# One core, a hybrid decoder layer: the loads of down's weights move from SyncE's queue to ScalarE's

## The chip, the cores and the metric

The kernel runs on one core of one Trainium2 chip. The metric is the device time of one execution in microseconds (us), lower is better. A profiled execution gives the trace from which all rows below come. A core has five engines with queues of their own: TensorE (PE), VectorE (DVE), ScalarE (ACT), GpSimd (POOL) and SyncE (SP); 16 DMA engines move data between the chip's memory (HBM) and the core's SBUF. A transfer is issued by an instruction in an engine's queue, here SP's or ACT's.

## The reference, cut to what matters

One layer on 256 tokens of width 1024: an SSD mixer, cross-attention into 256 memory rows, and a mixture of 32 experts, of which each token uses 4. The change touches the experts alone:

```python
def expert_block(args):
    xb, e = args
    gu = xb @ w_gate_up[e] + b_gate_up[e]            # 1024 x 2048 weights
    gate = jnp.minimum(gu[..., :D_FF], SWIGLU_LIMIT)
    up = jnp.clip(gu[..., D_FF:], -SWIGLU_LIMIT, SWIGLU_LIMIT)
    act = (up + 1.0) * (gate * jax.nn.sigmoid(gate * SWIGLU_ALPHA))
    return act @ w_down[e] + b_down[e]               # 1024 x 1024 weights
```

The rows of an expert's output are scaled by the router's gates and added to the tokens they belong to. All is float32: 8 MB of gate-up and 4 MB of down weights for each expert, 403 MB for the 32.

## The kernel before, in words

The mixer and the attention fill roughly the first 390 us. Their weights come in 2 MB pieces through three slots. Then come the 32 experts, one after the other, each with up to 64 tokens ("slots"); for experts with more than 64 tokens there is a list of extra rounds, which these inputs don't use.

Expert weights go through a ring of twelve 1 MB buffers in SBUF: eight for gate-up (`GP`), each with 128 rows of 8 KB, and four for down (`DP`), each with 256 rows of 4 KB. `load_gate_up` and `load_down` (lines 306 and 309) issue one piece each; landing raises a semaphore of that buffer, `g_ready[s]` or `d_ready[s]`. PE raises `gu_used` and `dn_used` after the last matmul of each piece, and that frees the buffer.

PE's order for expert e (`regular`, lines 788 to 798) is: transpose of the scatter matrix (line 714), gate_up(e) over eight pieces (726), gather of the tokens of e+1 (706), down(e-1) over four pieces (750), transposes of the gate-up sums of e (737), scatter of e-1 (760). So down runs one expert behind gate-up. down(e-1) needs `act` of e-1 and the scatter matrix in SBUF.

SP's loop (lines 361 to 364) follows the same order: the eight pieces of gate-up for the next expert, each as soon as the present expert's matmuls have freed its buffer, then the four pieces of down, each as soon as the piece of the expert before has been used. `wait_ge` stands before every issue, and the queue is served in order.

ACT's order for an expert (`regular`, lines 1044 to 1051) is: scatter matrix out of PSUM (`scatter_out`), the gate half of the sums (`gate_out`), the next expert's tokens (`tokens_out`), the former expert's down sums (`down_out`, which waits for all four of its pieces through `dn_used`), and the sigmoid of this expert. All are recorded as line 826, the helper's. ACT issues four small transfers at the start of the kernel and none later. DVE does the other half of the sums (1381), the clamps and products of SwiGLU (1388 to 1400, the last waits for the sigmoid) and the one-hot matrices.

```python
def reload_down(e, i, c):
    for s in range(DP):
        sp.wait_ge(dn_used, 2 * DP * i + (DP * (c - 1) + s + 1))
        load_down(sp, e, s)
```

Of the kernel before, what the change touches and what calls it, by code (L numbers as in the profile page):

```python
# [43 lines left out]
NE, TOPK = 32, 4  # L44
# [4 lines left out]
PAIRS = NE // 2  # L49
# [6 lines left out]
GP, DP = 8, 4  # L56
# [4 lines left out]
def build(nc, x, mem, mixer_norm, xattn_norm, mem_norm, ffn_norm, w_in, conv_w, conv_b, dt_bias, a_log,  # L61
          d_skip, ssd_norm, w_out, xa_w_q, xa_w_kv, xa_w_o, w_router, b_router, w_gate_up, b_gate_up,
          w_down, b_down, final_norm, out):
    with ExitStack() as ctx:
# [187 lines left out]
        def used(n):  # L252

            if n < W_Z:
                return u_ps, 2 * (n - W_U) + 2
            if n < KV_PIECE[0]:
                return z_ps, 2 * (n - W_Z) + 2
            if n in KV_PIECE:
                return kv_ps, 2 * KV_PIECE.index(n) + 2
            if n < W_Q:  # L260
                return wo_ps, (1, 2, 5, 6)[n - W_OUT]
            return (q_ps, 2 * (n - W_Q) + 2) if n < W_O else (wo_ps, 9 + n - W_O)
# [27 lines left out]
        def wpiece(n):  # L290
            return wslot[n % 3].rearrange("p (k n) -> p k n", k=KD)
# [7 lines left out]
        def dn_w(s):  # L299
            return slot(GP + s).rearrange("p (k n) -> p k n", k=2)  # L300
# [4 lines left out]
        def load_gate_up(sp, e, s):  # L305
            sp.dma_start(gu_w(s), gu_dram[e, s, :, :]).then_inc(g_ready[s], 16)  # L306

        def load_down(sp, e, s):
            sp.dma_start(dn_w(s), dn_dram[e, s, :, :, :]).then_inc(d_ready[s], 16)  # L309
# [4 lines left out]
        @block.sync  # L314
        def _(sp):
            for t in range(TC):
                sp.dma_start(h[:, t, :], x[P * t:P * (t + 1), :]).then_inc(ld_x, 16)
            for r0, v in ((16, mem_norm), (24, ssd_norm)):
                n = v.shape[0] // P
                sp.dma_start(rows_b[r0:r0 + n, :], v.rearrange("(c p) -> c p", p=P)).then_inc(ld_rows, 16)  # L320
            sp.wait_ge(ld_rows, 96)
            sp.dma_start(wpiece(0), pieces[0]).then_inc(w_ready[0], 16)
            sp.dma_start(wdt[:, :, :], w_in[:, 5120:5152].rearrange("(k p) n -> p k n", p=P)).then_inc(ld_wdt, 16)
            for n, v in enumerate((dt_bias, a_log, d_skip)):
                sp.dma_start(small[:, n, :], v.partition_broadcast(P)).then_inc(ld_small, 16)
            sp.dma_start(b_rt[:, :], b_router.partition_broadcast(P)).then_inc(ld_small, 16)
            sp.dma_start(bg_rows, b_gate_up.rearrange("e (f q) -> (e f) q", q=P).rearrange(
                "(n p) q -> p n q", p=P)).then_inc(ld_bg, 16)
            sp.dma_start(wpiece(1), pieces[1]).then_inc(w_ready[1], 16)
            sp.dma_start(vb[:, :, :], mem.rearrange("(t p) d -> p t d", p=P)).then_inc(ld_mem, 16)  # L330
            sp.dma_start(wpiece(2), pieces[2]).then_inc(w_ready[2], 16)
            sp.dma_start(wrt[:, :, :], w_router.rearrange("(k p) n -> p k n", p=P)).then_inc(ld_wrt, 16)
            for n in range(3, len(pieces)):
                signal, count = used(n - 3)
                sp.wait_ge(signal, count)
                sp.dma_start(wpiece(n), pieces[n]).then_inc(w_ready[n % 3], 16)
            sp.wait_ge(sc_ps, XH)
            sp.dma_start(g_ffn, ffn_norm.partition_broadcast(P)).then_inc(ld_g, 16)
            sp.wait_ge(pT_ps, XH)
            for s in range(GP):  # L340
                load_gate_up(sp, 0, s)
            sp.wait_ge(wo_ps, 10)
            for s in range(DP):
                load_down(sp, 0, s)
            sp.dma_start(bdn[0:NE, :], b_down).then_inc(ld_bdn, 16)
            sp.dma_start(g_fin, final_norm.partition_broadcast(P)).then_inc(ld_gf, 16)

            def reload_gate_up(e, i, c):

                for s in range(GP):  # L350
                    sp.wait_ge(gu_used, 2 * GP * i + (GP * (c - 1) + s + 1))
                    load_gate_up(sp, e, s)
# [7 lines that stand above are left out]
            reload_gate_up(1, 0, 1)  # L360
            with sp.Fori(0, PAIRS - 1, 1) as i:
                for c in range(2):
                    reload_gate_up(2 * i + (c + 2), i, c + 2)
                    reload_down(2 * i + (c + 1), i, c + 1)
            reload_down(NE - 1, PAIRS - 1, 1)
            sp.wait_ge(lst_ok, 1)
            extra = sp.value_load(lst_i[0:1, 32:33], min_val=0, max_val=MAX_EXTRA)
            with sp.Fori(0, EXTRA_PAIRS, 1) as q:
                with sp.If(extra > 2 * q):
                    for c in range(2):  # L370
                        e = sp.value_load(lst_i[0:1, ds(2 * q + (16 + c), 1)], min_val=0, max_val=NE - 1)
                        reload_gate_up(e, q, NE + c)
                        reload_down(e, q, NE + c)
            for t in range(TC):
                sp.wait_ge(o_ok, t + 1)
                sp.dma_start(out[P * t:P * (t + 1), :], h[:, t, :]).then_inc(ld_out, 16)
            sp.wait_ge(ld_out, 16 * TC)
# [446 lines left out]
        def _(act_):  # L824
            def fn(out_, in_, func, **kw):
                return nc.scalar.activation(out_, in_, func, **kw)  # L826
# [179 lines left out]
            def tokens_out(i, c, buf):  # L1006

                act_.wait_ge(gathered, 2 * i + (c + 1))
                fn(xs[:, buf, :, :], ps[3][:, :].rearrange("p (k s) -> p k s", k=KD), ACT.Copy).then_inc(xs_ok, 1)

            def scatter_out(i, c):

                act_.wait_ge(st_ps, 2 * i + (c + 1))
                fn(scatT[:, :], ps[2][:, 0:SEQ], ACT.Copy).then_inc(sT_ok, 1)

            def gate_out(i, c):

                act_.wait_ge(gu_used, 2 * GP * i + GP * (c + 1))
                fn(gus[:, 0:512], ps[0][:, :], ACT.Copy).then_inc(gus_act, 1)

            def sigmoid(i, c):

                act_.wait_ge(gate_b, 2 * i + (c + 1))
                fn(sg[:, :, :, :], gu[:, 0, :, :, :], ACT.Sigmoid, scale=ALPHA).then_inc(sg_ok, 1)

            def down_out(i, c):

                act_.wait_ge(dn_used, 2 * DP * i + DP * (c + 1))
                fn(ysb[:, :], ps[2][:, :], ACT.Copy).then_inc(y_ok, 1)
# [14 lines left out]
            def regular(i, c, buf, more=True):  # L1044

                scatter_out(i, c)
                gate_out(i, c)
                if more:
                    tokens_out(i, c + 1, 1 - buf)
                down_out(i, c - 1)  # L1050
                sigmoid(i, c)

            with act_.Fori(0, PAIRS - 1, 1) as i:
                regular(i, 1, 1)
                regular(i, 2, 0)
            regular(PAIRS - 1, 1, 1, False)
            scatter_out(PAIRS - 1, 2)
            down_out(PAIRS - 1, 1)
# [434 lines left out]
```

## Time and profile before

| what | value |
|---|---|
| time, median of 3 runs | 1374.69 us (1371.0 to 1376.38) |
| the profiled execution | 1370.06 us |
| its span, first to last instruction | 1368.3 us |
| PE busy | 1278.7 us, 93% of the span |
| DVE, ACT, POOL busy | 380.2, 247.4, 18.8 us |
| DMA | 454.24 MB, mean 332 GB/s |
| gate-up issues on SP | 256 of 1024 KB, median 20.1 us to landing |
| down issues on SP | 128 of 1024 KB, median 24.4 us to landing |
| mean granted TensorE clock | 0.98 |

The profile is one execution. Its own time differs from its span by what lies around the first and the last instruction, 1.8 us. Busy time counts an engine's instructions; waits, and the issues of transfers, are not in it. The time to landing runs from the start of the issue to the moment at which the whole piece has arrived.

### The profile page before, as it was taken

The numbers are of one execution on the slowest core, as the hardware profiler recorded it, in microseconds if no ns is written. First come the engines' busy times: TensorE is split into PE (matmuls) and PEld (weight loads), VectorE is DVE, ScalarE is ACT, GpSimd is POOL, SyncE is SP. The second block draws the span as 40 slices with busy tenths as digits, with TensorE's granted clock in tenths as the row PEclk, the third lists the DMA queues.
The fourth block names the chain that finished last, engine by engine and source line by source line (L and its number), as shares of the span: only waits on it lengthen the run. The fifth ranks groups of instructions, "written<-read, shape, count | busy, mean of one in ns | idle before, by whom it ended". The sixth has DMA issues, their size and how long they took to land.

```text
span 1368.3 us, 17022 instructions
## 1 busy us (share of the span) xinstructions
PE 1278.7 (93%) x6566; PEld 684.3 (50%) x6566; DVE 380.2 (28%) x746; ACT 247.4 (18%) x389; POOL 18.8 (1%) x33
## 2 busy tenths in 40 slices
PE   6999998989899999999999999999999999999984
PEld 6998775867654444444433433333344343333421
DVE  1885577343421121112111111211111122111112
ACT  2754225233301010001000000100000010000101
POOL 1000210000000000000000000000000000000000
PEclk9999999999878999999999999999999999999997
DMA  8454213332857999999999999999999999999993
GB/s 290 161 184 175 73 62 123 123 123 102 356 208 310 417 417 416 418 419 419 418 418 416 416 417 418 419 419 418 416 417 416 418 419 418 418 417 417 416 416 133
DMA packets 99187, 454.24 MB, mean 332 GB/s; under 512 B 9364, under 2 KB 10036, under 8 KB 66388
## 3 DMA queue, kind: packets, MB, share of 16 engines
q1 hardware_dynamic: 98976, 453.75, 82.3%
q8 instruction: 21, 0.34, 0.1%
q10 hardware_dynamic: 180, 0.07, 0.0%
q14 instruction: 10, 0.08, 0.0%
HBM read 452.74 MB, written 1.05 MB: 332 GB/s over the span
## 4 chain that ended last, share of the span: by engine, by line
PE 45%; DMA 32%; SPq 16%; DVE 3%; issue 2%; ACT 1%; DVEq 1%; ACTq 0%
DMA ring<-in_moe_w_gate_up 28%; PE ps L726 11%; SPq L306 9%; PE ps L750 6%; SPq L309 6%; PE ps L706 5%; PE ps L485 3%; PE ps L486 3%; PE ps L487 3%; PE ps L576 2%; PE ps L500 2%; PE ps L502 2%; PE ps L501 2%; DMA ring<-in_moe_w_down 2%; PE ps L580 1%
## 5 line engine op out<-in xcount | busy, mean ns | idle before, releaser
L726 PE MATMUL ps<-ring,wring 128*64 128x512 f32 x2048 | 464.9, 601 | 35.0 <-DMA ring<-in_moe_w_gate_up 33.4
L726 PEld LDWEIGHTS ps<-ring,wring 128*64 128x64 f32 x2048 | 142.0, 137 | 336.2 <-issue 230.2
L750 PE MATMUL ps<-ring,wring 128*64 128x512 f32 x1024 | 227.4, 596 | 3.7 <-DMA ring<-in_moe_w_down 2.5
L826 ACT ACTIVATE wring<-ps 128x512 f32<-128x512 f32 (+1 forms) x133 | 72.2, 544 | 832.5 <-PE ps L726 486.0
L1381 DVE COPY wring<-ps 128x512 f32<-128x512 f32 x32 | 22.1, 692 | 431.9 <-PE ps L726 431.9
L750 PEld LDWEIGHTS ps<-ring,wring 128*64 128x64 f32 x1024 | 70.4, 137 | 135.6 <-issue 121.5
L1388 DVE TENSOR_TENSOR wring<-ps,bguT 128x512 f32<-128x512 f32 x64 | 44.0, 688 | 332.6 <-PE ps L737 332.6
L706 PEld LDWEIGHTS ps<-wring 128*128 128x128 f32 x1024 | 120.0, 196 | 26.7 <-issue 25.2
L706 PE MATMUL ps<-wring 128*128 128x64 f32 x1024 | 124.4, 281 | 1.4 <-DVE wring L1367 1.4
L1117 DVE TENSOR_TENSOR wlo<-wring,lo_ring 128x2048 fp32r<-128x2048 f32 x26 | 58.8, 2288 | 41.9 <-ACT lo_ring L826 41.9
L760 PE MATMUL ps<-wring 64*128 64x512 f32 x256 | 63.6, 615 | 0.7 <-ACT wring L826 0.7
L826 ACT ACTIVATE lo_ring<-wring 128x2048 fp32r<-128x2048 f32 x26 | 49.0, 1916 | 34.4 <-DMA wring<-in_ssd_w_in 16.8
L502 PE MATMUL ps<-hi_ring,wlo 128*128 128x256 f32 x192 | 54.4, 283 | 0.0
L500 PE MATMUL ps<-hi_ring,lo_ring 128*128 128x256 f32 x128 | 36.6, 286 | 5.3 <-DVE act_lo L1281 3.5
L737 PEld LDWEIGHTS ps<-cst,wring 128*128 128x128 f32 x256 | 28.1, 143 | 25.2 <-issue 25.1
L486 PE MATMUL ps<-wlo,hi_ring 128*128 128x512 f32 x96 | 38.2, 398 | 0.0
L502 PEld LDWEIGHTS ps<-hi_ring,wlo 128*128 128x128 f32 x192 | 36.9, 192 | 0.0
L485 PE MATMUL ps<-lo_ring,hi_ring 128*128 128x512 f32 x80 | 32.6, 407 | 4.2 <-DVE hi_ring L1306 4.2
L737 PE MATMUL ps<-cst,wring 128*128 128x128 f32 x256 | 35.8, 284 | 0.0
L760 PEld LDWEIGHTS ps<-wring 64*128 64x128 f32 x256 | 22.1, 186 | 21.8 <-issue 20.3
L473 PE MATMUL ps<-mid,wring 128*128 128x256 f32 x128 | 29.5, 393 | 2.2 <-DMA wring<-in_ssd_w_in 2.2
L1184 DVE SCALAR_TENSOR_TENSOR ring<-ps,parT,ring 128x255 f32<-128x255 f32 (+2 forms) x72 | 31.1, 477 | 1.8
(234 smaller groups left out, 1067.9 us busy)
## 6 DMA issues: line engine op xcount, KB each, us to landing
ring<-in_moe_w_gate_up SPq DMA_DIRECT2D x256, 1024.0 KB, 20.1
ring<-in_moe_w_down SPq DMA_DIRECT2D x128, 1024.0 KB, 24.4
wring<-in_ssd_w_in SPq DMA_DIRECT2D x10, 2048.0 KB, 8.0
wring<-in_xa_w_kv SPq DMA_DIRECT2D x4, 2048.0 KB, 8.2
wring<-in_ssd_w_out SPq DMA_DIRECT2D x4, 2048.0 KB, 7.7
wring<-in_xa_w_q SPq DMA_DIRECT2D x2, 2048.0 KB, 7.9
wring<-in_xa_w_o SPq DMA_DIRECT2D x2, 2048.0 KB, 10.4
h<-in_x SPq DMA_DIRECT2D x2, 512.0 KB, 4.3
```

Of the source, the lines that this page charges most:

```text
L306: sp.dma_start(gu_w(s), gu_dram[e, s, :, :]).then_inc(g_ready[s], 16)
L309: sp.dma_start(dn_w(s), dn_dram[e, s, :, :, :]).then_inc(d_ready[s], 16)
L485: mm(ps[bank][:, :], xh[:, k0 + k, tok], wh, start=start and k == 0, stop=False)
L486: mm(ps[bank][:, :], xh[:, k0 + k, tok], wl, start=False, stop=False)
L500: mm(dst, wh[:, c0:c0 + P], x_hl[0][:, k, :], start=k == 0, stop=False)
L502: last = mm(dst, wl[:, c0:c0 + P], x_hl[0][:, k, :], start=False, stop=k == KD - 1)
L706: last = mm(ps[G_BANK][:, SLOTS * k:SLOTS * (k + 1)], xn[:, t, P * k:P * (k + 1)], onehot[:, buf, t, :], start=t == 0, stop=t == TC - 1)
L726: last = mm(ps[a][SLOTS * half:SLOTS * (half + 1), :], xs[:, buf, s, :], w[:, c0:c0 + 512], start=s == 0, stop=s == GP - 1)
L737: last = tr(ps[a][:, P * j:P * (j + 1)], gus[:, c0:c0 + P], ident)
L750: last = mm(ps[D_BANK][SLOTS * half:SLOTS * (half + 1), :], act[:, k, :], w[:, kk, 512 * half:512 * (half + 1)], start=k == 0, stop=k == K ...
L760: mm(ps[4 + 2 * half + t][:, :], scatT[r, P * t:P * (t + 1)], ysb[r, :], start=False, stop=True, skip_group_check=True)
L826: return nc.scalar.activation(out_, in_, func, **kw)
```

## The change

SP no longer issues the pieces of down in its main loop, and neither those of the last expert behind it. ACT issues them: behind `down_out` of expert e-1, and before the sigmoid of e, it issues the four pieces of down for e, without a wait of their own, since `down_out` has already waited until all four buffers are free. The first expert's down pieces and those of the extra rounds stay with SP.

```diff
@@ -361,8 +361,6 @@
             with sp.Fori(0, PAIRS - 1, 1) as i:
                 for c in range(2):
                     reload_gate_up(2 * i + (c + 2), i, c + 2)
-                    reload_down(2 * i + (c + 1), i, c + 1)
-            reload_down(NE - 1, PAIRS - 1, 1)
             sp.wait_ge(lst_ok, 1)
             extra = sp.value_load(lst_i[0:1, 32:33], min_val=0, max_val=MAX_EXTRA)
             with sp.Fori(0, EXTRA_PAIRS, 1) as q:
@@ -1048,6 +1046,8 @@
                 if more:
                     tokens_out(i, c + 1, 1 - buf)
                 down_out(i, c - 1)
+                for s in range(DP):
+                    load_down(act_, 2 * i + c, s)
                 sigmoid(i, c)
 
             with act_.Fori(0, PAIRS - 1, 1) as i:
```

## Rows read from the trace of the kernel before

**Rows 1.** The page's part 2, share of the DMA engines in 40 slices of the span.

```profile
DMA  8454213332857999999999999999999999999993
```

**Rows 2.** Windows of the span: length, busy us (instructions) of each engine, PEclk, DMA share, GB/s.

```profile
450.05:700.00 249.95, 248.35 (x1297) 108.52 (x1297) 45.56 (x99) 24.96 (x45) 0.00 (x0) 1.00 1.02 418
700.00:1000.00 300.00, 284.88 (x1456) 118.80 (x1454) 50.62 (x110) 28.05 (x50) 0.00 (x0) 1.00 1.02 418
```

**Rows 3.** PE's timeline, 440 to 482 us: start, length, line, operation, tiles, count.

```profile
442.63 7.09 PE L750 MATMUL ps<-ring,wring 128*64 128x512 f32 x32
...
453.01 13.95 PE L726 MATMUL ps<-ring,wring 128*64 128x512 f32 x64
466.89 3.79 PE L706 MATMUL ps<-wring 128*128 128x64 f32 x32
470.61 7.09 PE L750 MATMUL ps<-ring,wring 128*64 128x512 f32 x32
```

**Rows 4.** PE's timeline, 815 to 850 us; in brackets idle time before and what ended it.

```profile
827.58 8.80 PE L726 MATMUL ps<-ring,wring 128*64 128x512 f32 x40
836.77 1.94 PE L726 MATMUL ps<-ring,wring 128*64 128x512 f32 x8 [0.39 <-DMA ring<-in_moe_w_gate_up]
839.26 1.94 PE L726 MATMUL ps<-ring,wring 128*64 128x512 f32 x8 [0.56 <-DMA ring<-in_moe_w_gate_up]
...
847.32 3.23 PE L750 MATMUL ps<-ring,wring 128*64 128x512 f32 x14
```

**Rows 5.** SP's line 309 from 786 to 803 us: issue ns min/median/max, and landing.

```profile
L309 SPq DMA_DIRECT2D ring<-in_moe_w_down x4: 488/3654/4412, 789.3 to 798.8; - x4
...
DMA to landing us min/median/max: 23.1/24.9/25.8
```

**Rows 6.** SP's timeline, 440 to 482 us.

```profile
455.13 12.33 SPq L306 DMA_DIRECT2D ring<-in_moe_w_gate_up  x8
472.72 5.52 SPq L309 DMA_DIRECT2D ring<-in_moe_w_down  x4
```

**Rows 7.** Single issues at 397.5, 439.2 and 444.8 us, each with its landing.

```profile
L306 SPq DMA_DIRECT2D ring<-in_moe_w_gate_up x1: 334/334/334, 397.5 to 397.5; - x1
...
DMA to landing us min/median/max: 4.7/4.7/4.7
...
L306 SPq DMA_DIRECT2D ring<-in_moe_w_gate_up x1: 332/332/332, 439.2 to 439.2; - x1
...
DMA to landing us min/median/max: 10.9/10.9/10.9
...
L309 SPq DMA_DIRECT2D ring<-in_moe_w_down x1: 384/384/384, 444.8 to 444.8; - x1
...
DMA to landing us min/median/max: 7.9/7.9/7.9
```

**Rows 8.** ACT's timeline, 815 to 850 us.

```profile
824.37 0.60 ACT L826 ACTIVATE wring<-ps 128x512 f32<-128x512 f32 x1 [6.43 <-PE ps L750]
826.29 0.63 ACT L826 ACTIVATE wring<-wring 128x512 f32<-128x512 f32 x1 [1.33 <-DVE wring L1392]
827.67 0.38 ACT L826 ACTIVATE wring<-ps 128x256 f32<-128x256 f32 x1 [0.74 <-PE ps L714]
843.72 0.60 ACT L826 ACTIVATE wring<-ps 128x512 f32<-128x512 f32 x1 [15.67 <-PE ps L726]
```

**Rows 9.** DMA queues between 3 and 4 us (q1 SyncE's, q10 ScalarE's): packets, MB, share.

```profile
q1 hardware_dynamic: 97, 0.36, 88.9%
q10 hardware_dynamic: 98, 0.04, 15.0%
```

**Rows 10.** PE's timeline, 1296 us to the end.

```profile
1299.12 7.09 PE L750 MATMUL ps<-ring,wring 128*64 128x512 f32 x32
...
1323.85 1.94 PE L726 MATMUL ps<-ring,wring 128*64 128x512 f32 x8 [0.54 <-DMA ring<-in_moe_w_gate_up]
1326.49 1.94 PE L750 MATMUL ps<-ring,wring 128*64 128x512 f32 x8 [0.71 <-DMA ring<-in_moe_w_down]
...
1334.08 1.94 PE L750 MATMUL ps<-ring,wring 128*64 128x512 f32 x8 [0.62 <-DMA ring<-in_moe_w_down]
...
1340.55 7.09 PE L750 MATMUL ps<-ring,wring 128*64 128x512 f32 x32 [1.22 <-DVE wring L1400]
```

## Prediction, before the changed kernel ran

> **What bounds the kernel now.** Below, G(e) and D(e) are the eight gate-up and the four down pieces of expert e, 1 MB each, and "down(e)" is the stretch of matmuls that uses D(e). I read the page's row of DMA shares first: from the thirteenth slice to the last but one every digit is 9 [rows 1]. The windows then give 1.02 as the share and 418 GB/s as the rate, both before 700 us and after it, while PE falls from all but 1.6 us of the first window to 284.88 of 300 us [rows 2]. So the transfers don't stop at 700 us, but PE starts to wait there.
>
> PE's timeline shows the two regimes. Early, one expert takes PE 477.70 - 449.72 = 28.0 us between the ends of two downs: 3.3 of small work, 13.95 gate-up, 3.7 gather, 7.1 down, without a gap [rows 3]. Later the gate-up matmuls come in bursts 2.49 us apart, each released by a DMA [rows 4]. At the end down does the same, (1334.08 - 1326.49) / 3 = 2.53 us apart [rows 10]; I take 2.55 for a down piece. One expert's bytes thus take 8 x 2.49 + 4 x 2.55 = 19.9 + 10.2 = 30.1 us, 2.1 more than PE's 28.0. **The bound is the DMA engines, busy without a pause from before 450 us [rows 2] until the last expert's down.** Whatever the change does to the order of the bytes costs nothing by itself; what costs is a pause of the engines.
>
> SyncE looks like a bottleneck but isn't one. In the bound regime a down piece holds its queue for a median of 3.65 us and lands 23.1 to 25.8 us after its issue [rows 5], while early, with fewer pieces ahead, an issue takes 0.38 us [rows 7]. The queue is simply full; nobody waits for the issue, since 23 us are some nine pieces that lie ahead of each.
>
> **The change, part by part.** Removed: 31 x 4 waits and issues on SP. SP now issues G alone, at most eight pieces outstanding, so its 3.65 us stalls go. I cost this at nothing: a G piece that enters a full queue earlier lands no earlier. If the queue were ever empty it would be worth up to the stall.
>
> Added: 124 issues on ScalarE. In each expert four stand after the down eviction and before the sigmoid. On an unfilled queue four take 4 x 0.38 = 1.5 us [rows 7]; on a full one up to 4 x 4.4 = 17.6 us [rows 5]. Now ACT evicts at 824.37, does the sigmoid at 826.29 and is next needed at 827.67 and 843.72 [rows 8]. With 1.5 us nothing moves. What waits behind it: the sigmoid, DVE's last product, and with it act for down, whose matmuls start 23 us after the eviction [rows 4]; then scatT, for the same down; then the gate half's eviction at 843.72. The long bound would end at 842.6 and leave 1.1 us for a sigmoid and an eviction that take 1.0, so even it would barely show. I take 1.5 us and nothing on the path, for ACT's queue never holds more than four pieces.
>
> Delayed: D. Piece 0 goes out today at 472.72, 2.1 us after down starts, and the four within 5.5 us, the last just after the end [rows 3, 6]. After the change all four wait for the end T of down, the semaphore (0.1) and the eviction (0.60 [rows 8]). A piece on an empty queue lands 4.7 us after issue [rows 7], 2.5 of it transfer, so 2.2 is start-up. D's bytes thus begin to move at T + 0.7 + 2.2 = T + 2.9. (If ScalarE's queue issues before the eviction ends it is T + 2.3.) That matters only where less than 2.9 us of gate-up transfer is queued at T; call this remainder x.
>
> *Head.* T = 449.72 for expert 0. G(2) has all landed at 439.2 + 10.9 = 450.1, so x = 0.4, and D(1) piece 0 lands today at 444.8 + 7.9 = 452.7, straight behind it [rows 7]. Afterwards it lands at T + 2.9 + 2.55 = 455.2. **Cost 2.5 us**, once: from the next expert on x grows by 2.1 each time.
>
> *Middle.* Two queues now feed the same DMA engines, and today's timeline shows how they share in one microsecond only: between 3 and 4 us, ScalarE's queue moved 98 packets and SP's 97 [rows 9], though SP's carried 0.36 MB and the other 0.04. So turns, not bytes, are equal. What a turn holds for G and D is not shown. A G row is 8 KB, a D row 4 KB, which by single rows gives G two bytes for each of D; if a turn is as many bytes for both, they go equal. The Trainium skill's DMA: Bandwidth & Descriptors, Queues, rings and completion order, says that an engine goes round-robin between queues and drains a whole packet of several descriptors each time; by it no order of issue is kept between SP and ScalarE, and the equal counts above agree. Its section Issuing engines are not separate DMA queues says that spreading issues gains no bandwidth; by it the sum has no gain. If the packet of the first section were all that one piece gives an engine, the same 64 KB for both, that rule would mean equal shares and the 1384 below; no run shows how large it is here.
>
> Two to one: D needs 3 x 10.2 = 30.6 us while G is queued. G(e+2) pieces are asked for from 2.1 us after gate-up starts [rows 3, 6] and can move from T + 3.3 + 2.1 + 2.2 = about T + 7.7. From x = 5: G runs dry at 2.9 + 2.1 x 1.5 = 6.1, D runs alone to 7.7, has had 2.7 and ends at 7.7 + 3 x 7.5 = 30.2; the last down piece ends at 32.1; G(e+2) has had 15.0 + 1.9, so x = 19.9 - 16.9 = 3.0. From x = 3: D ends at 24.2, PE needs its 28.1, and x = 5.0 again. Rounds of 32.1 and 28.1 average 30.1: the engines stay fed, barely, as 3.0 is just over 2.9. Equal shares: D lands by T + 23.3, G's last at T + 2x - 2.9, and the next T is 1.9 + 3.7 + 7.1 later, T + 2x + 9.8; for rounds of 30.1, x = 10.1. Either way **the middle costs nothing**, but PE now waits for D or for G in place of running ahead, and x falls.
>
> *Tail.* Here the small x is paid. Expert 29's down ends today at T29 = 1299.12 + 7.09 = 1306.2, G(31) is complete at 1323.8, so x = 17.6; down(30) ends at 1336.0 and down(31) at 1347.6, 11.6 later, partly waiting for DVE [rows 10]. Afterwards D(31) can't be asked for before T30: it is complete at T30 + 0.7 + 2.2 + 10.2 = 13.1 and used 1.9 later, at T30 + 15.0, 3.4 more than today, with the engines idle. And T29 comes later, since more bytes must have moved by then. With two to one (x about 4): T29 = 1306.2 + 2.5 + 13.6 = 1322.3; then PE's own 3.3 + 13.95 + 7.1 = 24.4 gives T30 = 1346.7, and down(31) ends at 1361.7: **14.1 us late**. With equal shares (x = 10.1): T29 = 1316.2, T30 = 26.4 later (G(31) lands at T29 + 17.3, no gather), 1342.6, end 1357.6: 10.0 late.
>
> **The sum**: 2.5 in the head, 0 in the middle, 11.6 in the tail (8.2 from x, 3.4 from the late D(31)). On the profiled execution's 1370.06 us (span 1368.3) that gives 1384.2. The three runs shown have their median 4.6 above the profiled one; I keep most of that and say **1388 us**, against a median of 1374.69. I take two to one, because the row sizes are what the trace has; equal shares would give 1384.
>
> **Rivals.** *1, the middle starves as well.* With two to one every second round has x = 3.0 against 2.9. A slower start-up, or a G share above two, makes x fall short, and the engines pause up to 2.9 us in each of some 22 late rounds, or D lands so late that down waits longer than G(e+2), with only eight slots, can fill. At 0.7 to 1.4 us a round: 15 to 31 more, 1403 to 1419. For it: the margin of 0.1. Against it: a longer round also refills x.
>
> *2, order kept.* If older requests were served first, G(e+1) would stay ahead of D(e), x would stay 17.6, and only 2.5 + 3.4 = 5.9 us would be lost: 1380. Against it the equal counts of rows 9.
>
> *3, faster.* A D piece takes 0.06 us longer than a G piece for the same bytes, with 16 rows for each of the 16 engines where G has 8; so a row seems to cost 0.06 / 8 us beyond its bytes, 0.06 for G and 0.12 for D. If another queue's work hid that cost entirely, a G piece would take 2.43 and a D piece 2.43, and an expert 29.2: 0.9 x 31 = 28 less than the forecast, or 1360. It decides where the round is shorter than 30.1 by 14.1 / 30 = 0.5 us, that is above 425 GB/s where rows 2 show 418. Against it: the share is 1.02 already. The same place could also lose: a rate 1% lower costs 9 us.
>
> *4, nothing happens.* If D's issue landed in time in head and tail for a reason not seen, or other effects gave 11 us back, the time stays near 1375.
>
> **How the numbers follow.** About 0.5% (7 us) is what a measurement of this kernel can tell from no change, so the border is 1381.6. Forecast, with shares from equal to two to one: 0.53, 1382 to 1394. Starved middle, or a lower rate: 0.25, all slower. Order kept: 0.11, on the border, halved. Faster: 0.05. Nothing: 0.06. That makes slower 0.83, same 0.12, faster 0.05. The range leaves out the faster case, most of the unchanged one and the far end of the starved one: 1379 to 1412.
>
> **What would show it.** D issues on ACTq of about 0.4 us each, and no SP issue over 1 us. Middle windows still at 1.0 and 418 GB/s. D(1) piece 0 landing near 455. At T29 only 3 to 10 us of G(31) left, D(31) issued after T30 and landing 10 to 13 us later, with a DMA gap between. Wrong if: down matmuls in the middle are never later than gate-up's data (order kept); the middle's rate is below 415 or above 425; or ACT's issues take 4 us each and its evictions slip.

## The result, and the profile after

The changed kernel takes 1387.89 us, the median of four runs (1385.43 to 1390.18), against 1374.99 for the kernel before (also four): a ratio of 1.0098, 95% interval 1.0071 to 1.0126. In a second comparison with more runs (E1 below) it is 1.0122 (1.0103 to 1.0140). So the change costs about 1%, 13 to 17 us. The difference of the medians and the one by the ratio lie up to 1.3 us apart in the experiments below, which give both. The profiled execution took 1385.43 us against 1370.06, its span is 1383.6 us against 1368.3: 15.3 longer. In the new kernel the gate-up matmuls have line 724 and down's 748, two less than before.

First the page of the changed kernel: DMA shares by slice, then the queues (packets, MB, share).

```profile
DMA  8455123333857999999999999999999999999973
...
q1 hardware_dynamic: 65248, 323.71, 57.9%
q10 hardware_dynamic: 33908, 130.10, 23.6%
```

The row of nines answers to [rows 1]; its last digit but one is a 7 now, where the kernel before had a 9: the engines run dry before the end. q10 is ScalarE's queue: 130 MB of down weights have moved there. Next the windows, with the columns of [rows 2]:

```profile
450.00:700.00 250.00, 237.44 (x1202) 102.47 (x1200) 44.86 (x98) 23.94 (x43) 0.00 (x0) 0.97 1.00 410
700.00:1000.00 300.00, 286.38 (x1462) 124.06 (x1460) 50.62 (x110) 28.03 (x50) 0.00 (x0) 0.97 1.02 417
1000.00:1300.00 300.00, 284.19 (x1457) 122.78 (x1455) 49.34 (x106) 28.05 (x50) 0.00 (x0) 0.98 1.02 418
```

From 700 us on the DMA engines are as busy as before, 417 and 418 GB/s. Before 700 us they lose some: 410 instead of 418. The prediction named a middle rate below 415 as a sign of being wrong. This window also holds the pause of the head (14 GB/s between 450 and 452 us); from 490 to 700 us alone the rate is 413, so in these first rounds there are short pauses that the prediction did not have. Then ACT's timeline and the issues of both queues:

```profile
1022.50 0.60 ACT L824 ACTIVATE wring<-ps 128x512 f32<-128x512 f32 x1 [6.43 <-PE ps L748]
1022.63 1.99 ACTq L309 DMA_DIRECT2D ring<-in_moe_w_down  x4
1024.67 0.63 ACT L824 ACTIVATE wring<-wring 128x512 f32<-128x512 f32 x1 [1.57 <-DVE wring L1392]
```

```profile
L306 SPq DMA_DIRECT2D ring<-in_moe_w_gate_up x81: 332/333/333, 699.7 to 999.9; - x81
```

Four issues take ACT 2.0 us, and no SP issue takes over 0.333 us, where a down piece held SP for a median of 3.65 [rows 5]. The first issue starts at 1022.63, 0.13 us after the eviction began and before its end at 1023.10: here the queue does not wait for the engine to finish. The sigmoid keeps its place behind DVE's line 1392, about as in [rows 8].

How the pieces land: three issues of ScalarE's queue in one expert, and PE beside them.

```profile
L309 ACTq DMA_DIRECT2D ring<-in_moe_w_down x3: 379/379/380, 1023.2 to 1024.2; - x3
...
DMA to landing us min/median/max: 13.0/19.9/26.7
```

```profile
997.76 13.96 PE L724 MATMUL ps<-ring,wring 128*64 128x512 f32 x64
...
1015.36 7.09 PE L748 MATMUL ps<-ring,wring 128*64 128x512 f32 x32
...
1025.71 13.96 PE L724 MATMUL ps<-ring,wring 128*64 128x512 f32 x64
...
1043.31 5.37 PE L748 MATMUL ps<-ring,wring 128*64 128x512 f32 x24
1050.97 1.94 PE L748 MATMUL ps<-ring,wring 128*64 128x512 f32 x8 [2.30 <-DMA ring<-in_moe_w_down]
```

The three were issued at 1023.17, 1023.71 and 1024.24 and landed 13.0, 19.9 and 26.7 us later: at 1036.2, 1043.6 and 1050.9, so 7.4 and 7.3 us apart, three times the 2.49 of a gate-up piece. While both queues have work, from 1040 to 1050 us, they move nearly as many packets as each other, and SyncE's twice the bytes:

```profile
q1 hardware_dynamic: 375, 2.81, 67.4%
q10 hardware_dynamic: 365, 1.40, 35.1%
```

In exchange gate-up, which PE waited for in [rows 4], now comes in time: 13.96 us without a gap in both rounds. PE waits for down's last piece instead, 2.30 us here. The ends of down stand at 1022.45 and 1052.91: a round of 30.5, and the one before, 994.50 to 1022.45, is 27.95. And the end of the kernel, which answers to [rows 10]:

```profile
1316.69 7.09 PE L748 MATMUL ps<-ring,wring 128*64 128x512 f32 x32
...
1327.02 13.96 PE L724 MATMUL ps<-ring,wring 128*64 128x512 f32 x64
1340.80 7.04 PE L748 MATMUL ps<-ring,wring 128*64 128x512 f32 x32
...
1353.07 5.35 PE L748 MATMUL ps<-ring,wring 128*64 128x512 f32 x16 [1.92 <-DMA ring<-in_moe_w_down]
1358.76 1.94 PE L748 MATMUL ps<-ring,wring 128*64 128x512 f32 x8 [0.34 <-DMA ring<-in_moe_w_down]
1361.27 1.94 PE L748 MATMUL ps<-ring,wring 128*64 128x512 f32 x8 [0.57 <-DMA ring<-in_moe_w_down]
```

down(29) ends at 1323.78, 17.6 us later than before, down(30) at 1347.84, 11.8 later, and down(31) at 1363.20, 15.6 later. down(31) is now served piece by piece from the DMA engines, 15.4 us behind down(30), where it took 11.6 and waited only for its activations. D(31) is issued from 1347.9 us on, and from 1342 to 1346 us nothing moves (0 GB/s): that pause is the 7 in the row of shares.

### The profile page after: what moved, and what is told of

Same layout as the page of the kernel before. It is cut to its first block, busy times and chain, and to the rows that moved or that the text cites. A ratio compares the mean times of both kernels' runs of the same rounds, so it can differ in the third digit from the quotient of the medians.

```text
span 1383.6 us, 16904 instructions
## 1 busy us (share of the span) xinstructions
PE 1288.1 (93%) x6566; PEld 698.9 (51%) x6566; DVE 380.3 (27%) x746; ACT 247.3 (18%) x389; POOL 18.8 (1%) x33
## 4 chain that ended last, share of the span: by engine, by line
PE 61%; DMA 31%; DVE 3%; ACTq 2%; issue 1%; ACT 1%; SPq 1%; DVEq 1%
DMA ring<-in_moe_w_down 29%; PE ps L724 18%; PE ps L748 12%; PE ps L704 5%; PE ps L483 3%; PE ps L484 3%; PE ps L485 3%; PE ps L758 2%; PE ps L574 2%; PE ps L498 2%; PE ps L499 2%; PE ps L500 2%; PE ps L735 2%; ACTq L309 1%; DMA wring<-in_ssd_w_in 1%
## 5 line engine op out<-in xcount | busy, mean ns | idle before, releaser
L724 PEld LDWEIGHTS ps<-ring,wring 128*64 128x64 f32 x2048 | 149.2, 138 | 280.6 <-issue 280.0
L748 PEld LDWEIGHTS ps<-ring,wring 128*64 128x64 f32 x1024 | 72.3, 143 | 187.2 <-issue 124.1
L735 PE MATMUL ps<-cst,wring 128*128 128x128 f32 x256 | 38.8, 300 | 0.0
## 6 DMA issues: line engine op xcount, KB each, us to landing
ring<-in_moe_w_gate_up SPq DMA_DIRECT2D x256, 1024.0 KB, 14.1
wring<-in_xa_w_o SPq DMA_DIRECT2D x2, 2048.0 KB, 10.3
```

Source lines behind the costliest of these rows:

```text
L724: last = mm(ps[a][SLOTS * half:SLOTS * (half + 1), :], xs[:, buf, s, :], w[:, c0:c0 + 512], start=s == 0, stop=s == GP - 1)
L735: last = tr(ps[a][:, P * j:P * (j + 1)], gus[:, c0:c0 + P], ident)
L748: last = mm(ps[D_BANK][SLOTS * half:SLOTS * (half + 1), :], act[:, k, :], w[:, kk, 512 * half:512 * (half + 1)], start=k == 0, stop=k == K ...
```

## The experiments

Two explanations were set against each other. The main one is that of the prediction: two queues share the DMA engines, so that down takes bytes that gate-up needs first, and x (the gate-up transfer still queued at the end of a down) falls; that is paid for once, at the end, together with a late start in the head and a late D(31). The rival: it is the late issue that costs, in each round, and the second queue is harmless.

### E1: the changed kernel again

No edit.

> The changed kernel once more, as the measure for the three beside it. Main theory (D's own queue shares two to one with gate-up, so that the gate-up queued at the end T of a down, x, falls from 17 us to 2 to 9 us; this is paid once at the end, with 2.5 us in the head and 3.4 for the late D(31)): 13 to 16 us over the kernel before, rounds of 28 to 35 us averaging 30.1. Rival (D issued late starves the DMA engines in every round): the same total, but windows of the middle below 415 GB/s.

Measured: 1389.04 us against 1371.71, 17.3 us more; ratio 1.0122 (1.0103 to 1.0140), which is 16.7. That is just over the upper end of 13 to 16. The rounds of its trace lie between 27.9 and 34.7 us; from the end of down(9) at 722.31 to that of down(29) at 1327.54 they average 605.23 / 20 = 30.26. The rival wanted windows of the middle below 415 GB/s: they show 418 (700 to 1000 us) and 417 (1000 to 1300 us). Only the window from 450 to 700 us, which holds the head's pause, shows 411.

### E2: late, but in one queue

The edit is on `reload_down` of the kernel before.

```diff
-                for s in range(DP):
-                    sp.wait_ge(dn_used, 2 * DP * i + (DP * (c - 1) + s + 1))
-                    load_down(sp, e, s)
+                sp.wait_ge(dn_used, 2 * DP * i + DP * c)
+                for s in range(DP):
+                    load_down(sp, e, s)
```

> SP issues everything as in the kernel before, but the four pieces of D(e) all wait until the last piece of down(e-1) is used. One queue, so order is kept. Main theory: only head (2.5) and D(31) (3.4) are lost, 5 to 7 us over the kernel before; rounds stay at 30.1 each, x stays 17.4. Rival (late issue is the whole loss): 13 us or more, as with the change.

Measured: 1380.04 us, 8.3 us more; ratio 1.0051 (1.0032 to 1.0070), which is 7.0. That is the upper end of 5 to 7, or just over it. PE's timeline at the end:

```profile
1307.16 7.09 PE L750 MATMUL ps<-ring,wring 128*64 128x512 f32 x32
...
1326.74 1.94 PE L726 MATMUL ps<-ring,wring 128*64 128x512 f32 x8 [0.44 <-DMA ring<-in_moe_w_gate_up]
1329.42 1.94 PE L726 MATMUL ps<-ring,wring 128*64 128x512 f32 x8 [0.74 <-DMA ring<-in_moe_w_gate_up]
1331.91 1.94 PE L726 MATMUL ps<-ring,wring 128*64 128x512 f32 x8 [0.55 <-DMA ring<-in_moe_w_gate_up]
...
1342.07 1.94 PE L750 MATMUL ps<-ring,wring 128*64 128x512 f32 x8 [0.55 <-DMA ring<-in_moe_w_down]
...
1349.15 1.94 PE L750 MATMUL ps<-ring,wring 128*64 128x512 f32 x8 [1.83 <-DMA ring<-in_moe_w_down]
...
1357.37 1.94 PE L750 MATMUL ps<-ring,wring 128*64 128x512 f32 x8 [0.57 <-DMA ring<-in_moe_w_down]
```

The middle is that of the kernel before: the last gate-up pieces come 2.5 to 2.7 us apart, released by the DMA, the round from 1314.25 (end of down(29)) is again DMA-bound, and down(30) ends 29.8 later. down(31) ends at 1359.31, 15.3 behind down(30) instead of 11.6: **3.7 us for the late D(31)**. In the head, between 440 and 490 us, 19.71 MB moved instead of 20.88, which is 2.8 us. The late issue alone is worth no more than half of the change's loss: 8.3 of 17.3 us by the medians, 7.0 of 16.7 by the ratios. The rival, which wanted 13 us or more, falls.

### E3: two queues, nothing late

```diff
-                down_out(i, c - 1)
                 for s in range(DP):
+                    act_.wait_ge(dn_used, 2 * DP * i + (DP * (c - 1) + s + 1))
                     load_down(act_, 2 * i + c, s)
+                down_out(i, c - 1)
```

The eviction `down_out` now stands behind the four issues.

> ACT issues D, each piece as soon as its own buffer is free, ahead of the eviction. Two queues, nothing late. Main theory: no loss in the head, none for D(31); x still falls to about 4, so T29 comes 17.6 - 4 = 13.6 late and the last round is 5.4 shorter: 7 to 9 us over the kernel before, with D landings 7.3 us apart while gate-up is queued. Rival (late issue is the whole loss): within 2 us of the kernel before.

Measured: 1377.52 us, 5.8 us more; ratio 1.0036 (1.0023 to 1.0049), which is 4.9. That is below the 7 to 9 expected and outside the rival's 2. The four D pieces issued from 1008.0 to 1013.5 land from 11.5 to 27.8 us after their issues, 7.3 us apart as expected. PE at the end:

```profile
1312.93 1.94 PE L748 MATMUL ps<-ring,wring 128*64 128x512 f32 x8 [0.47 <-DMA ring<-in_moe_w_down]
...
1333.56 7.04 PE L748 MATMUL ps<-ring,wring 128*64 128x512 f32 x32
...
1345.12 7.09 PE L748 MATMUL ps<-ring,wring 128*64 128x512 f32 x32 [1.05 <-DVE wring L1401]
```

down(29) ends at 1314.87, 8.7 later than in the kernel before, the next round takes 25.7 instead of 29.8, and down(31) follows after 11.6, as before, at 1352.21: 4.6 late, of which 0.4 were there at the end of down(0), and the rest comes from the bytes that moved earlier than they were needed. After T29 12.91 MB are left here, 16.16 in the kernel before: 3.25 MB, or 7.8 us, make down(29) late, and the shorter round gives 4.1 of them back. The mechanism is as expected, its size was not: I had carried x = 4 over from the late case. With D issued during the former down, D is well on its way at T. The last gate-up piece still lands 16.9 us after T here, two thirds of which are its own transfer: x = 11.3.

### E4: the change, with D(31) early

```diff
+            reload_down(NE - 1, PAIRS - 1, 1)
             sp.wait_ge(lst_ok, 1)
...
-                for s in range(DP):
+                for s in range(DP if more else 0):
                     load_down(act_, 2 * i + c, s)
```

> The changed kernel, but D(31) alone is issued by SP again, each piece as soon as its buffer is free. Main theory: down(31) ends 11.6 us after down(30) instead of 15.4, so 3 to 4 us less than the changed kernel, 10 to 12 over the kernel before; T30 unchanged. Rival (down(31) is bound by its activations and not by D(31)): no gain.

Measured: 1383.80 us, 12.1 over the kernel before; ratio 1.0086 (1.0072 to 1.0100), which is 11.8; and 5.2 below E1, which was measured beside it.

```profile
1340.93 7.04 PE L749 MATMUL ps<-ring,wring 128*64 128x512 f32 x32
...
1352.50 7.09 PE L749 MATMUL ps<-ring,wring 128*64 128x512 f32 x32 [1.22 <-DVE wring L1401]
```

down(30) ends at 1347.97, within 0.2 of the changed kernel's, and down(31) 11.6 later, at 1359.59, no longer 15.4: 3.8 us, where the sum had 3.4. The rival (no gain) falls. The medians say 5.2, with intervals that nearly touch, 1.0100 and 1.0103; what makes the rest of the 5.2 was not looked into.

### E5 and E6: 8 KB rows for down, in one queue and in two

Down's pieces are laid out as 128 rows of 8 KB instead of 256 of 4 KB. Each partition takes two neighbouring rows of w_down; the transposes of the gate-up sums and those of the biases take every second column, so that activations and weights still meet.

```diff
-        dn_dram = w_down.rearrange("e (s k p) n -> e s p k n", p=P, k=2)
+        dn_dram = w_down.rearrange("e (s p k) n -> e s p (k n)", p=P, k=2)
...
-                        c0 = 512 * a + P * j
-                        last = tr(ps[a][:, P * j:P * (j + 1)], gus[:, c0:c0 + P], ident)
+                        last = tr(ps[a][:, P * j:P * (j + 1)],
+                                  gus.rearrange("p (b f k) -> p b k f", b=4, k=2)[:, 2 * a + j // 2, j % 2, :], ident)
```

The same edit changes the load itself (one row of 8 KB for each partition) and the layout of the biases; these lines are left out here. E5 is that edit on the kernel before, E6 on the changed one.

> The kernel before (one queue), with down's weights laid out in SBUF as 128 rows of 8 KB for each piece instead of 256 of 4 KB: each partition takes two neighbouring rows of w_down, and the transposes and the biases take every second column to match. Main theory (a row costs about 0.0075 us per engine beyond its bytes, and the DMA engines are the bound): a D piece takes 2.49 us instead of 2.55, a round 29.9 instead of 30.1, 31 experts give 6 to 8 us: 1363 to 1367. Rival (the 0.06 has to do with the tensor, not with the rows): no change, or slower by the strided transposes.

> The changed kernel with the same 8 KB rows for down. If a turn between the queues is one row of either (main theory), G and D now share equally: D pieces land 4.9 to 5.1 us apart while gate-up is queued, not 7.3, x settles near 10, and the kernel is 8 to 11 us over e5_one_queue_8k_rows. Rival (ScalarE's queue has a third whatever the rows, or a turn is of equal bytes): D pieces stay 7.3 us apart, and it is 13 to 17 us over e5.

Measured: E5 1363.02 us against 1372.38, 9.4 us less; ratio 0.9941 (0.9927 to 0.9955), which is 8.1: **faster than both kernels**. E6 1373.43 us, ratio 1.0007 (0.9994 to 1.0021), 10.4 over E5. E5's window and its last round:

```profile
700.00:1000.00 300.00, 289.24 (x1474) 120.76 (x1469) 50.64 (x110) 28.05 (x50) 0.00 (x0) 1.00 1.01 422
```

```profile
1291.38 7.09 PE L751 MATMUL ps<-ring,wring 128*64 128x512 f32 x32
...
1318.25 1.94 PE L751 MATMUL ps<-ring,wring 128*64 128x512 f32 x8 [0.64 <-DMA ring<-in_moe_w_down]
...
1325.64 1.94 PE L751 MATMUL ps<-ring,wring 128*64 128x512 f32 x8 [0.54 <-DMA ring<-in_moe_w_down]
...
1332.20 7.09 PE L751 MATMUL ps<-ring,wring 128*64 128x512 f32 x32 [1.18 <-DVE wring L1402]
```

422 GB/s instead of 418, and the down pieces of the last round come (1325.64 - 1318.25) / 3 = 2.46 us apart, as gate-up's do. The last three downs end at 1298.47, 1327.58 and 1339.29; the last is 8.3 us earlier than in the kernel before. The time lies at the low edge of what was expected, since a round of the middle takes 29.8, not 29.9. The rival of E5 falls. The packets of the trace before show the price of a row directly: from 500 to 1200 us one of 4 KB takes 163 ns on average, one of 8 KB 314, so two short rows cost 12 ns more than a long one. Then three issues of ScalarE's queue in E6, and PE at its end:

```profile
L310 ACTq DMA_DIRECT2D ring<-in_moe_w_down x3: 339/339/340, 1249.6 to 1250.6; - x3
...
DMA to landing us min/median/max: 13.5/18.0/22.5
```

```profile
1301.47 7.09 PE L749 MATMUL ps<-ring,wring 128*64 128x512 f32 x32
...
1327.46 7.04 PE L749 MATMUL ps<-ring,wring 128*64 128x512 f32 x32
...
1347.61 1.94 PE L749 MATMUL ps<-ring,wring 128*64 128x512 f32 x8 [0.52 <-DMA ring<-in_moe_w_down]
```

The three pieces, issued 0.50 us apart, land 13.5, 18.0 and 22.5 us after their issues, so 5.0 us apart, no longer 7.3. **A turn between the queues is thus the same number of rows of either**: 8 against 4 KB is two to one, 8 against 8 is even. ScalarE's queue has no smaller share of its own. That the number is one is not in the shares, but in the packets of the changed kernel's trace. From 1040 to 1050 us their starts and durations fit together into 16 chains (one for each DMA engine, an inference from the times), and in nine of ten cases the queue changes after a single packet, which is one row. x at T29 is about 9.5 in E6: G(31) lands 17.0 us after it, of which 2.1 alone and the rest at one half. down(29) ends at 1308.56 (10.1 after E5's), down(30) at 1334.50 (6.9), down(31) at 1349.55 (10.3).

### E7 and E8: sixteen experts

Both kernels with the first 16 experts only; the other 16 are left out.

```diff
-PAIRS = NE // 2
+PAIRS = NE // 4
...
-            reload_down(NE - 1, PAIRS - 1, 1)
+            reload_down(2 * PAIRS - 1, PAIRS - 1, 1)
```

(The second line stands in E7 alone.)

> The kernel before with the first 16 experts only; the other 16 are left out. The measure for the next. 16 rounds of 30.1 less: about 890.

> The changed kernel with the first 16 experts only. Main theory (the loss is paid once, in head and tail, while the rounds average 30.1): 12 to 17 us over e7_before_16_experts, as with 32 experts. Rival (each round costs a little): half of the 32 experts' loss, 7 to 8 us.

Measured: 889.40 and 904.37 us, four runs each, 888.28 to 891.42 and 901.99 to 908.56: 15.0 us more, as with 32 experts (12.9 and 17.3 in the two comparisons). So the rounds of the other sixteen experts cost nothing that these runs can tell. What the rounds of the first sixteen cost is not seen here, since both comparisons hold them.

## Why the prediction was right

It said 1388 us, from 14.1 over the profiled kernel before and 3.8 for the gap between the profiled execution and the median. The median is 1387.89, and the traces differ by 15.3. The mechanism holds. That the number is met to 0.1 us is luck: the second comparison gives 17.3 us more instead of 12.9, and two terms were too small and one too large by about as much. The bytes that the DMA engines moved, by the profile of the kernel before and of the changed one in turn: from 440 to 490 us, from 490 to 1200 us, and from T29 to the end.

```profile
DMA packets 3892, 20.88 MB, mean 418 GB/s; under 512 B 320, under 2 KB 320, under 8 KB 2368
DMA packets 3462, 19.55 MB, mean 391 GB/s; under 512 B 287, under 2 KB 287, under 8 KB 1869
...
DMA packets 52506, 296.59 MB, mean 418 GB/s; under 512 B 4527, under 2 KB 4527, under 8 KB 28079
DMA packets 52586, 295.45 MB, mean 416 GB/s; under 512 B 4513, under 2 KB 4513, under 8 KB 28531
...
DMA packets 3393, 16.16 MB, mean 257 GB/s; under 512 B 272, under 2 KB 272, under 8 KB 2576
DMA packets 2772, 11.61 MB, mean 193 GB/s; under 512 B 206, under 2 KB 206, under 8 KB 2510
```

By the prediction's steps, at 418 GB/s:

- **Added issues on ScalarE: right.** Four take 2.0 us, 1.5 was said, and nothing shifts. That they don't wait for the eviction's end was left open. The first is issued 0.2 us after T, so that with the forecast's 2.2 us of start-up D begins to move at T + 2.4, not 2.9.
- **Head, 2.5: too small.** D(1) piece 0 is issued at 450.87 and lands 4.9 later, at 455.8, where 455.2 was forecast from a T that now is 450.67. The loss is larger than that landing: between 440 and 490 us 1.33 MB less moved, or 3.2 us. The pause is longer than forecast at its front: the rate falls to 388 GB/s from 440 to 450 us, is 14 from 450 to 452 and 268 from 452 to 454. So the engines had begun to run dry before T, where the forecast had x = 0.4 after it. That T itself is 0.95 later is not the experts' doing; the parts before 450 us vary by that and more between traces (T is 450.0 in E5, 454.0 in E2).
- **Sharing two to one: right**, and by the mechanism named: rows take turns. The D pieces land 7.3 us apart, and the shares are even once the rows are even (E6). The Trainium skill's page DMA: Bandwidth & Descriptors says, under Queues, rings and completion order, that an engine takes turns at packets of several descriptors. The turns are confirmed, but not their size: were they of 64 KB, the shares would have been even with 4 KB rows too, and the packets' times show turns of a single row here. The measurement decides.
- **Middle, 0: too small.** Rounds go from 27.94 to 35.42 us and average 30.1, at 417 and 418 GB/s from 700 us on. Some x fall below the start-up: the round that ends at 693.98 finds 1.5 us of gate-up left, and the engines pause (184 GB/s from 694 to 696 us). Between 490 and 1200 us 1.14 MB less moved: 2.7 us, of which 2.3 before 700 us. The prediction's margin of 0.1 us, named under its first rival, did not hold in each round.
- **Tail by x, 8.2: mechanism right, too large.** The last piece of G(31) is issued at 1313.21 and lands 18.0 later, 7.4 us after T29, of which 2.4 alone and 5.0 at two thirds, so x = 5.7 instead of about 4. By the bytes, 11.61 MB are left after T29 where 16.16 were left before: 4.55 MB or 10.9 us later, where the forecast had 13.6. (17.6 - 5.7 = 11.9 by the landings, which hold more than the transfer alone.) The last round takes 24.06 instead of 29.81, which gives 5.75 back: 5.1.
- **Late D(31), 3.4: right.** 15.36 - 11.61 = 3.75 in the trace, 3.7 in E2 and 3.8 in E4.

The measured terms, 0.95 + 3.2 + 2.7 + 5.1 + 3.75 = 15.7, meet the 15.6 by which down(31) is late. Of the rivals, order kept is E2, where it costs 7.0 to 8.3 us (5.9 was said) and where each of its two terms shows by itself; the two queues don't keep it. The starved middle exists in single rounds, nearly all before 700 us, and costs 2.7 us and not the 15 to 31 of that rival; E8 can't price it, since its sixteen experts hold those rounds too. The faster one needed a rate above 425 GB/s; it stayed at 418. Its premise, though, a price for each row, was worth more than the change: E5. The case of equal shares, forecast as 10.0 late at the end and 6.6 at down(30), is what E6 shows against E5: 10.3 and 6.9.

The parts don't add up from E2 and E3: by the ratios 7.0 + 4.9 is 11.9, and E1, measured beside them, 16.7. The traces tell of two reasons: two queues with an early D leave x at 11.3, with a late one at 5.7; and the pauses of the middle need both, a late D and a low x (E2 and E3 hold 418 GB/s from 490 to 1200 us). How the rest divides was not measured.

## What to carry to other kernels

When the DMA engines are the bound and always busy, the order in which bytes arrive costs nothing in the middle. What counts is how much of what is needed next is still queued when the work runs out. So moving a stream to a second queue was a choice about priority here, not about bandwidth (418 GB/s with either). The two queues took turns by rows: the stream with the shorter rows got the smaller share (7.3 us for a piece with 4 KB rows, 5.0 with 8 KB), and a stream that wasn't needed yet took bytes from the one that was. Before issues are moved about, look at the rows themselves: making down's twice as long gave 0.6% here, while each of the queue arrangements lost.

## What was not expected

TensorE's clock. After the longest waits for down's last piece, the piece that follows runs slowly. PE and two windows of the changed kernel:

```profile
679.41 5.59 PE L748 MATMUL ps<-ring,wring 128*64 128x512 f32 x24
690.30 3.68 PE L748 MATMUL ps<-ring,wring 128*64 128x512 f32 x8 [5.30 <-DMA ring<-in_moe_w_down]
```

```profile
680.00:686.00 6.00, 5.00 (x24) 1.24 (x20) 0.00 (x0) 0.12 (x1) 0.00 (x0) 1.00 1.02 418
686.00:694.00 8.00, 3.70 (x9) 0.86 (x10) 0.00 (x0) 0.00 (x0) 0.00 (x0) 0.62 1.02 422
```

After 5.30 us of waiting the last eight matmuls take 3.68 us where others take 1.94, with a granted clock of 0.62 over the 8 us around: in part of them it was at 1.2 instead of 2.4 GHz. It may be one reason why x, once low, falls further: T comes 1.7 us later while gate-up goes on landing. No run has the change without it. The kernel before had no such dip between 450 and 1345 us, and E2 and E3 show a granted clock of 1.00 in all windows between 450 and 1300 us, where the changed kernel shows 0.97 and 0.98. So their losses owe it nothing; of what the change loses beyond them, the clock may have a part. In E6 one dip came at a worse place:

```profile
908.57 2.69 PE L725 MATMUL ps<-ring,wring 128*64 128x512 f32 x8 [2.18 <-DMA ring<-in_moe_w_gate_up]
911.19 7.09 PE L705 MATMUL ps<-wring 128*128 128x64 f32 x32
918.21 9.59 PE L749 MATMUL ps<-ring,wring 128*64 128x512 f32 x32
```

After 12.2 us of work and a wait of 2.18 us the gather takes 7.09 us where it takes 3.79, down 9.59 where it takes 7.09, and that round 37.0 us; the granted clock is 0.58 from 907 to 923 us. No run was made to price it. E6 lies 10.4 us over E5, within the 8 to 11 expected without a dip, so its total shows little of it.
